# Final norm of a two-layer trunk: tokens in parts of 384 and 128 columns, last square added by TensorE, gains applied on ScalarE

## The reference

```python
def rms_norm(x, g):
    y = x * lax.rsqrt(jnp.mean(x * x, axis=-1, keepdims=True) + EPS)
    return y * g

x = x + g2 * (jnp.square(jax.nn.relu(h2 @ w_up[l])) @ w_down[l])   # last layer
return rms_norm(x, final_g)
```

## Time and profile before

| | |
|---|---|
| three runs | 1161.89, 1161.94, 1162.43 us; median 1161.94 |
| profiled execution | 1161.66 us |
| its span | 1159.8 us |
| TensorE matmuls busy | 1131.3 us, 98% |
| VectorE, ScalarE, GpSimd busy | 863.9 (74%), 580.2 (50%), 172.1 us (15%) |
| granted clock over the span | 0.998 |
| HBM read, written | 160.06 MB, 2.10 MB |

### The profile page before, as it was taken

The page is one execution under the profiler, slowest core; times in us unless marked ns, Lnnn a source line. Parts: engine busy times, 40 slices in busy tenths (PEclk is TensorE's granted clock), DMA queues, the critical chain, the costliest instruction groups (busy, mean ns, idle before and its releaser), DMA issues.

```text
span 1159.8 us, 19123 instructions
## 1 busy us (share of the span) xinstructions
PE 1131.3 (98%) x6682; PEld 1006.8 (87%) x6682; DVE 863.9 (74%) x1315; ACT 580.2 (50%) x981; POOL 172.1 (15%) x132
## 2 busy tenths in 40 slices
PE   4999999999999999999999999999999999999996
PEld 2788888998989989989998888889989989999896
DVE  6967898679788687685677688886897575675754
ACT  5655544247445454454444555434555454544632
POOL 4484010320000000000215800004000000000003
PEclk9999999999999999999999999999999999999999
DMA  9774334624353353433345433452334232232312
GB/s 350 308 290 146 127 109 145 218 74 141 132 161 114 126 162 127 141 117 105 128 152 210 179 112 127 146 213 95 119 100 128 85 107 99 90 126 73 103 60 74
DMA packets 47061, 162.87 MB, mean 140 GB/s; under 512 B 5536, under 2 KB 7712, under 8 KB 46752
## 3 DMA queue, kind: packets, MB, share of 16 engines
q1 hardware_dynamic: 47008, 162.18, 40.2%
HBM read 160.06 MB, written 2.10 MB: 140 GB/s over the span
## 4 chain that ended last, share of the span: by engine, by line
PE 93%; DVE 3%; ACT 1%; DMA 1%; issue 1%; SPq 1%; POOL 0%; POOLq 0%; DVEq 0%; ACTq 0%
PE ps L368 21%; PE ps L369 21%; PE ps L370 21%; PE ps L524 8%; PE ps L526 8%; PE ps L525 8%; PE ps L621 1%; PE ps L410 1%; DVE h_lo L1092 1%; DMA w_raw<-weights 1%; PE ps L604 1%; PE ps L411 1%; PE ps L412 1%; DVE x L1129 1%; DVE x L1157 0%
## 5 line engine op out<-in xcount | busy, mean ns | idle before, releaser
L1013 DVE TENSOR_TENSOR w_lo<-w_raw,w_hi 128x1024 fp32r<-128x1024 f32 (+1 forms) x190 | 225.5, 1188 | 179.8 <-ACT w_hi L701 178.1
L701 ACT CAST w_hi<-w_raw 128x1024 fp32r<-128x1024 f32 (+1 forms) x190 | 189.2, 997 | 77.2 <-PE ps L370 66.6
L368 PE MATMUL ps<-u_hi,w_hi 128*128 128x512 f32 (+1 forms) x576 | 211.5, 367 | 0.0
L369 PE MATMUL ps<-u_lo,w_hi 128*128 128x512 f32 (+1 forms) x576 | 210.9, 366 | 0.0
L370 PE MATMUL ps<-u_hi,w_lo 128*128 128x512 f32 (+1 forms) x576 | 210.6, 366 | 0.0
L368 PE MATMUL ps<-h_hi,w_hi 128*128 128x512 f32 (+1 forms) x528 | 194.4, 368 | 0.8 <-DVE h_lo L1092 0.8
L370 PE MATMUL ps<-h_hi,w_lo 128*128 128x512 f32 (+1 forms) x528 | 192.0, 364 | 0.0
L369 PE MATMUL ps<-h_lo,w_hi 128*128 128x512 f32 (+1 forms) x528 | 192.0, 364 | 0.0
L1603 POOL TENSOR_TENSOR ssum<-ssum,buf_a 128x256 f32<-128x256 f32 (+1 forms) x56 | 51.7, 923 | 774.2 <-ACT buf_a L729 771.5
L1157 DVE SCALAR_TENSOR_TENSOR x<-ps,mod,x 128x512 f32<-128x512 f32 (+1 forms) x168 | 105.4, 669 | 34.5 <-PE ps L370 34.5
L370 PEld LDWEIGHTS ps<-u_hi,w_lo 128*128 128x128 f32 x576 | 108.7, 189 | 17.6
(11 more groups left out here) (196 smaller groups left out, 2324.8 us busy)
## 6 DMA issues: line engine op xcount, KB each, us to landing
w_raw<-weights SPq DMA_DIRECT2D x200, 512.0 KB, 3.4
ada_raw<-ada SPq DMA_DIRECT2D x80, 512.0 KB, 4.9
arena<-ada SPq DMA_DIRECT2D x16, 512.0 KB, 15.2
x<-xT SPq DMA_DIRECT2D x2, 1024.0 KB, 6.8
tab<-tables SPq DMA_DIRECT2D x2, 1024.0 KB, 14.5
outT<-x SPq DMA_DIRECT2D x8, 256.0 KB, 2.3
tab<-tables SPq DMA_DIRECT2D x1, 512.0 KB, 15.3
ident<-identity SPq DMA_DIRECT2D x1, 64.0 KB, 2.0
```

Of the source, the lines that this page charges most:

```text
L368: nc.tensor.matmul(out, wh, hi, start=first, stop=False, skip_group_check=True)
L369: nc.tensor.matmul(out, wh, lo, start=False, stop=False, skip_group_check=True)
L701: nc.scalar.copy(w_hi[:, j, cols], w_raw[:, j, cols]).then_inc(w_hi_done, 1)
L1013: nc.vector.tensor_tensor(w_lo[:, j, cols], w_raw[:, j, cols], w_hi[:, j, cols].bitcast(F32), ALU.subtract).then_inc(w_lo_done, 1)
```

## The change

Only the end of the last layer and the final norm change. The token parts are 384 and 128 columns (PARTS). The first layer keeps its halves. GpSimd adds seven squares a part; the eighth (slot 1 of buf_a) is multiplied by the column of 1/1024 on TensorE and added in PSUM. ScalarE, behind each square, writes x times the final gain into x_gained; VectorE then multiplies two to four tiles of x_gained at once by the spread value. The second spread goes to bank 0. Stores are of two tiles in part 0 (393 KB, rows of 1536 bytes) and of four in part 1 (262 KB, rows of 512 bytes). The core of the diff:

```diff
+PARTS = (slice(0, 3 * P), slice(3 * P, T))
+PART_TILES = ((0, 1, 2), (3,))
+        LAST_RMS = 0
@@ SyncE
-            for half, at in enumerate(HALVES):
-                for k in range(0, KT, 2):
-                    sp.wait_ge(out_ready, half * KT + k + 2)
-                    sp.dma_start(outT[k:k + 2, :, at].rearrange("k p t -> p k t"), x[:, k:k + 2, at]
-                                 ).then_inc(out_done, 16)
+            for part, tiles in ((0, 2), (1, 4)):
+                for k in range(0, KT, tiles):
+                    sp.wait_ge(out_ready, part * 4 + k // tiles + 1)
+                    sp.dma_start(outT[k:k + tiles, :, PARTS[part]].rearrange("k p t -> p k t"),
+                                 x[:, k:k + tiles, PARTS[part]]).then_inc(out_done, 16)
@@ TensorE
+            def last_mean(n, part, added):
+                pe.wait_ge(ssum_added, added + 2)
+                for t in PART_TILES[part]:
+                    nc.tensor.matmul(ps[:, STAT, t:t + 1], ssum[:, t * P:(t + 1) * P], mean_d[:],
+                                     start=t == PART_TILES[part][0], stop=False, skip_group_check=True)
+                pe.wait_ge(sq_ready, DEPTH * SQ - KT + part * KT)
+                for t in PART_TILES[part]:
+                    mm = nc.tensor.matmul(ps[:, STAT, t:t + 1], buf_a[:, 1, t * P:(t + 1) * P], mean_d[:],
+                                          start=False, stop=True, skip_group_check=True)
+                mm.then_inc(stat_ps, 1)
...
+                            down_half(j, half, ed + (2 + ED_LAST), PARTS[half])
+                            if half and j == 0:
+                                last_mean(n, 0, added + KT - 1)
+                            if half and j == 1:
+                                spread(n, 0, PARTS[0])
...
-            mean_squares(2 * DEPTH, 1, DEPTH * SQ)
-            pe.wait_ge(out_ready, KT)
-            spread(2 * DEPTH, 1, HALVES[1])
+            last_mean(2 * DEPTH, 1, DEPTH * SQ - 2)
+            pe.wait_ge(norm_r, DEPTH * 8 + 2)
+            nc.tensor.matmul(ps[:, LAST_RMS, PARTS[1]], ones[:], ssum[:, PARTS[1]], start=True, stop=True).then_inc(rinv_ps, 1)
@@ ScalarE
+                def last_square(part, m):
+                    at = PARTS[part]
+                    act.wait_ge(evac_dve, l * ED + (2 + ED_LAST + part * KT + m + 1))
+                    if m > 1:
+                        act.wait_ge(ssum_added, added + part * (KT - 1) + m + 1)
+                    nc.scalar.activation(buf_a[:, m % 2, at], x[:, m, at], ACT.Square).then_inc(sq_ready, 1)
+                    nc.scalar.activation(x_gained[:, m, at], x[:, m, at], ACT.Copy, scale=fin_g[:, m:m + 1]
+                                         ).then_inc(xg_ready, 1)
...
+                    for m in range(KT):
+                        last_square(0, m)
+                    last_square(1, 0)
+                    last_square(1, 1)
+                    last_root(0)
+                    for m in range(2, KT):
+                        last_square(1, m)
+                    last_root(1)
@@ VectorE
+            def final(part, k0, k1):
+                at = PARTS[part]
+                dve.wait_ge(xg_ready, part * KT + k1)
+                dve.wait_ge(rinv_ps, 4 * DEPTH + part)
+                nc.vector.tensor_tensor(x[:, k0:k1, at], x_gained[:, k0:k1, at],
+                                        ps[:, LAST_RMS if part else RMS, at].unsqueeze(1)
+                                        .to_broadcast([P, k1 - k0, at.stop - at.start]),
+                                        ALU.mult).then_inc(out_ready, 1)
...
+                    down_rest(0, PARTS[1])
+                    last_scale(0)
+                    down_rest(1, PARTS[1])
+                    final(0, 0, 2)
+                    down_rest(2, PARTS[1])
+                    final(0, 2, 4)
+                    down_rest(3, PARTS[1])
+                    final(0, 4, 6)
+                    last_scale(1)
+                    final(0, 6, 8)
+                    final(1, 0, 4)
+                    final(1, 4, 8)
@@ GpSimd
+                    for part, at in enumerate(PARTS):
+                        for m in range(KT - 1):
+                            pool.wait_ge(sq_ready, added + part * KT + m + 1)
+                            pool.wait_ge(ssum_added, added + part * (KT - 1) + m + 2)
+                            nc.gpsimd.tensor_tensor(ssum[:, at], ssum[:, at], buf_a[:, m % 2, at], ALU.add
+                                                    ).then_inc(ssum_added, 1)
```

More of the change, by code:

```diff
@@ L109, in trunk @@
         xr_all = view("xr_all", [P, KT, T])
+        over[0] = t_at
+        x_gained = view("x_gained", [P, KT, T])
         over[0] = t_at + 2 * D * 4
@@ L225, in trunk @@
         gm_ready = sem("gm_ready")
+        xg_ready = sem("xg_ready")
         xr_ready = sem("xr_ready")
@@ L353, in _ @@
                     load_step(l, 24, 0, 0)
-            for half, at in enumerate(HALVES):
-                for k in range(0, KT, 2):
-                    sp.wait_ge(out_ready, half * KT + k + 2)
-                    sp.dma_start(outT[k:k + 2, :, at].rearrange("k p t -> p k t"), x[:, k:k + 2, at]
-                                 ).then_inc(out_done, 16)
-            sp.wait_ge(out_done, 16 * KT)
+            for part, tiles in ((0, 2), (1, 4)):
[3 more added lines that the diff above has]
+                                 x[:, k:k + tiles, PARTS[part]]).then_inc(out_done, 16)
+            sp.wait_ge(out_done, 16 * 6)
         @block.tensor
@@ L499, in down, with down_half @@
                     mm.then_inc(pe_unit, 1)
-            def down_half(j, half, evac):
+            def last_mean(n, part, added):
[8 more added lines that the diff above has]
+                mm.then_inc(stat_ps, 1)
+            def down_half(j, half, evac, at):
                 for m in (2 * j, 2 * j + 1):
@@ L510, in down_half @@
                         mm = three(bank, j, CHUNK * (m % 2) + k, u_hi[:, CHUNK + k, :], u_lo[:, CHUNK + k, :],
-                                   k == 0, k == CHUNK - 1, HALVES[half])
+                                   k == 0, k == CHUNK - 1, at)
                     if half and m % 2:
@@ L679, in _ @@
                             pe.wait_ge(w_lo_done, u0 + (U_LAST + j + SLOTS + 1))
[L680 to L684, removed]
+                        if l < DEPTH - 1:
+                            down_half(j, half, ed + (2 + ED_LAST), HALVES[half])
+                            if half and j == 0:
+                                mean_squares(n, 0, added + KT)
+                            if half and j == 1:
+                                spread(n, 0, HALVES[0])
+                        else:
+                            down_half(j, half, ed + (2 + ED_LAST), PARTS[half])
+                            if half and j == 0:
+                                last_mean(n, 0, added + KT - 1)
+                            if half and j == 1:
+                                spread(n, 0, PARTS[0])
                 if l < DEPTH - 1:
                     v_step(u0 + UNITS, xs + XS, n, added + SQ_MLP)
-            mean_squares(2 * DEPTH, 1, DEPTH * SQ)
-            pe.wait_ge(out_ready, KT)
-            spread(2 * DEPTH, 1, HALVES[1])
+            last_mean(2 * DEPTH, 1, DEPTH * SQ - 2)
+            pe.wait_ge(norm_r, DEPTH * 8 + 2)
+            nc.tensor.matmul(ps[:, LAST_RMS, PARTS[1]], ones[:], ssum[:, PARTS[1]], start=True, stop=True).then_inc(rinv_ps, 1)
         @block.scalar
@@ L994, in down_squares, with last_root @@
                     down_square(1, 2 * j + 1)
-                for m in range(KT):
-                    down_square(0, m)
+                def last_square(part, m):
[6 more added lines that the diff above has]
+                                         ).then_inc(xg_ready, 1)
+                def last_root(part):
+                    act.wait_ge(stat_ps, DEPTH * 4 + part)
+                    t = slice(PART_TILES[part][0], PART_TILES[part][-1] + 1)
+                    nc.scalar.activation(std[:, t], ps[:, STAT, t], ACT.Sqrt, bias=eps[:, 0:1]).then_inc(norm_std, 1)
                 if l < DEPTH - 1:
+                    for m in range(KT):
+                        down_square(0, m)
                     between(l, 24, l * 2 + 2, 0, down_squares)
[L1000 to L1005, removed]
+                else:
+                    act.wait_ge(fin_in, 16)
+                    act.wait_ge(ssum_added, added + 2)
+                    for m in range(KT):
+                        last_square(0, m)
[5 more added lines that the diff above has]
+                    last_root(1)
         @block.vector
@@ L1068, in norm_scale, with last_scale @@
                                         ).then_inc(norm_r, 1)
+            def last_scale(part):
+                t = slice(PART_TILES[part][0], PART_TILES[part][-1] + 1)
+                tiles = len(PART_TILES[part])
+                dve.wait_ge(norm_std, DEPTH * 4 + part)
```

(25 more changed lines are left out.)

## The result

The changed kernel takes 1170.65 us (median of four, 1170.02 to 1171.37) against 1161.91 in the same comparison: ratio 1.0075, interval 1.0062 to 1.0088. It is slower by 8.7 us, where +2.6 was forecast with a range up to 1166.3.

The account below looks back on a forecast made before the run. The prediction took TensorE, 93% of the chain that ended last, to bound the kernel, with scalings and stores in the tail. TensorE's +5.4 us and the tail's -2.85 gave +2.55, so 1164.5 us, range 1162.2 to 1166.3.

Parts of the forecast that it names:

- rival B: Part 1's 128-column products leave the array partly empty, the granted clock falls: +10.4 us, 1174.9; chance 6%.
- a clock under 1.00 ahead of the tail: Listed sign of a wrong forecast: granted clock below 1.00 (2.4 GHz) before the end stretch after the last matmul.
- Part 0, +5.15: TensorE's 96 products of the first part, 384 columns each: 16.66 us instead of 11.51.
- Part 1, -0.85: TensorE's second part, 128 columns: 95 steps take 10.55 us where 256 columns took 11.39.
- floor of 0.11: Weight loads bound 128-column products on TensorE: 0.111 us a step, between 0.108 and 0.115.
- Rival A: Weight loads overlap in part 1, pace 0.066 us: 4.3 us less, 1160.2, not slower; chance 10%.
- The mean, +0.88: Part 0's mean on TensorE takes 12 single-column passes against 4, 8 x 0.11 us.
- The waits put at nothing: TensorE's wait for part 0's last square, and delays on other engines beside its stream: no cost.
- The spread, +0.22: Part 0's spread on TensorE costs 0.64 us for 384 columns, where 256 cost 0.42.
- The tail: From the last matmul's start s: scalings over at s+4.35, store data end at s+6.94; -2.85 us.
- The term for rows of 512 bytes: Final stores: twice the packets cost 0.15 us, between nothing and 1.6.
- The sum at full clock, +2.55: Whole kernel: TensorE's +5.4 us less 2.85 in the tail, with the granted clock at 1.00.

Follow-up runs that it names:

- the split: The kernel before with only its last down projection, norm and stores in parts of 384 and 128 columns: 1164.67 us, ratio 1.0025.
- the split with 12 passes: The kernel before with only the parts of 384 and 128 columns, its first mean computed twice: 1171.12 us, ratio 1.0078.
- two wide tiles: The changed kernel with 256 columns for tiles 2 and 3 of part 1 only: 1165.26 us, ratio 1.0027.

## Why the prediction was wrong, point by point

The direction was right and most terms of the sum were. The step that failed is rival B: "128 columns at a step of 0.11 leave the array partly empty" was set against "the window that holds the four passes stayed at 1.00, but they are short", and 6 in 100 followed. The whole forecast of part 1, 95 steps of 0.111, took a clock of 1.00 for granted; the runs showed 0.50 from the middle of part 1 on, at 0.213 a step. The prediction had named a clock under 1.00 ahead of the tail as a sign of being wrong.

- Part 0, +5.15: 16.66 us measured, exact.
- Part 1, -0.85, floor of 0.11: 0.112 measured while the clock was 1.00, in a stream of 128 columns as in three instructions. Rival A is refuted: only the first pair (1141.95, 1142.01) is closer, as in the head stage.
- The mean, +0.88: 12 passes cost 1.34. But they were costed as time alone. Together with 128 columns around them they brought the clock down, which was the decisive thing about them. That was in neither the sum nor the rivals: B blamed the columns and thought the passes too short to matter, and with 128 columns and 6 passes (the split) the clock stood.
- The waits put at nothing cost nothing: the six passes on the last square follow the first six at 1145.22, 0.64 later, which is six steps of 0.11, with no idle time.
- The spread, +0.22: right at full clock (0.65 for 384 columns with 256 in the second part, 0.64 forecast).
- The tail: s+4.35 and s+6.94 forecast, s+4.32 and about s+7.0 measured at full clock. The term for rows of 512 bytes was 0.15; at 285 GB/s the last 524 KB take 1.84 instead of 1.57, 0.27.
- The sum at full clock, +2.55. The changed kernel with 6 passes is 1.6 above the kernel before; six passes more at 0.11 make that 2.3. With 256 columns in the second part it is 3.23, less 0.86 for 95 steps of 0.120 instead of 0.111: 2.4. The arithmetic holds; both are worked out from other kernels, since the changed one was never seen at full clock.
- Rival B's price, +10.4, was too high because the clock fell only halfway through part 1. From the fall on, in the profiled execution: the first spread, 1148.49 to 1150.09 less two steps of 0.11, 1.38 instead of 0.64, 0.7; then 46 steps to 1159.91 at 0.213 instead of 0.112, 4.7. The last product is 5.3 late. The last passes and the last spread (0.60 and 0.80 against 0.40 and 0.49) are 0.5 longer, of which 0.4 shows in the span. That accounts for the 5.7 between this execution's span (1168.1) and the forecast one (1162.4). The median, 1170.65, is 0.6 above this execution, the fastest of the four; the other three were not profiled.

What brings the clock down is shown as far as the pairs of kernels go: 6 against 12 passes turn it, in the split alone and in the changed kernel, and 256 against 128 columns turn it with the passes kept. What the engine did before each of the three falls in the dense stretch (the changed kernel, the split with 12 passes, two wide tiles) was alike: products of 128 columns, 12 single-column passes, a few more products, and no idle time. The Trainium skill ("TensorE: Matmul & The Clock Gate", section "HAM oscillation — how this bites in real kernels") looks for gaps in which TensorE waits. Here there is none: PE is busy 6.65 of 6.65 us before the fall, as it is 6.40 of 6.40 in the two kernels with 6 passes that kept the clock. So the busy time of the profile did not tell them apart. How much more than six passes it needs, and whether their standing in a row matters, was not tried.

## What to carry to other kernels

Before narrowing matmuls, look up in the trace what the narrowest ones cost: here 384 + 128 columns cost 0.173 + 0.112 where 256 + 256 cost 0.240, because the weight load sets a floor, so a short last part must earn that back in the tail. And cost small matmuls twice, as time and as a risk to the clock of everything dense behind them: eight more passes cost 0.9 us among 256 columns, and six more cost 6.4 us among 128. When two edits are each worth little, time them together as well.

## What the runs showed of the hardware that I had not expected

- The granted clock halved with TensorE busy all the time: 2.1 us (two wide tiles), 2.3 us (the split with 12 passes) and 4.0 us (the changed kernel) after the mean's first pass. The times behind it scatter: 1170.0 to 1171.9 in the eight runs of the two kernels that lost the clock for good, 1162.96 to 1163.64 in the ten with 6 passes in the changed kernel.
- Once down it stayed down through the 48 products of 128 columns left in the changed kernel, 10 us, and came back 3.4 us later where the products behind the fall had 256 columns.
- At 0.50 the step of a 128-column product is 0.213 instead of 0.112, and its weight loads too start 0.213 apart: the floor under narrow products scales with the clock. Products of 256 columns take the same 0.213 there (two wide tiles), where at full clock they take 0.120.
- Stores with rows of 512 bytes ran at about 285 GB/s where rows of 1024 ran at 335 and, with parts of 256, at about 345.
